# Latent attention: ScalarE copies a turn's probabilities ahead of the next chunk's exponentials; the output stage sums its squares amid the first tile's products

## The reference

```python
s = jnp.einsum('bhqd,bhkd->bhqk', qb, kh) * scale
s = jnp.where(key_idx[None, :] <= q_idx[:, None], s, -jnp.inf)
p = jax.nn.softmax(s, axis=-1)
return jnp.einsum('bhqk,bhkd->bhqd', p, vh)
```

```python
mixed = jnp.concatenate([rms_norm_2(attn, attn_out_norm), rms_norm_2(lru, lru_out_norm)], axis=-1)
x = x + gate1 * (mixed @ w_out)
```

## Time and profile before

| | |
|---|---|
| median of 3 runs | 3761.67 us (3759.36 to 3768.54) |
| the profiled execution's own time | 3749.46 us |
| its span in the trace | 3747.6 us |
| PE busy | 3513.6 us, 94% |
| VectorE busy | 1692.7 us, 45% |
| ScalarE busy | 1037.1 us, 28% |
| GpSimd busy | 988.4 us, 26% |
| latent attention, 2352 to 2768 us: PE busy | 391.20 of 416 us |
| GpSimd busy in the same stretch | 220.10 of 416 us |
| first experts' gather after routing | 3106.49 us |

### The profile page before, as it was taken

One profiled execution on the slowest core, in us unless ns is written; L12 is line 12 of the kernel. 1 busy time (PEld: TensorE's weight loads), 2 busy tenths in 40 slices (PEclk: granted clock), 3 DMA queues, 4 the chain that ended last, 5 costly groups with the idle time before them and its releaser, 6 DMA issues. The chain is left out here.

```text
span 3747.6 us, 33237 instructions
## 1 busy us (share of the span) xinstructions
PE 3513.6 (94%) x11453; PEld 1838.4 (49%) x11453; DVE 1692.7 (45%) x4081; ACT 1037.1 (28%) x2543; POOL 988.4 (26%) x1362
## 2 busy tenths in 40 slices
PE   4999999999999999999999989999989978999997
PEld 3754455555445544444444445555555544444443
DVE  4666433343354763346665557443444452221221
ACT  3122222211100550012244446433322222222221
POOL 0277777500000780000000006555520001112111
PEclk7999999999999999999999989999999988999999
DMA  3134445434253103232211000001012226999997
GB/s 137 58 128 147 164 147 167 152 99 134 91 179 130 35 24 129 84 122 69 94 42 35 12 11 1 1 1 68 1 58 96 74 93 250 323 329 333 332 326 234
DMA packets 115563, 459.96 MB, mean 123 GB/s; under 512 B 13587, under 2 KB 41107, under 8 KB 103356
## 3 DMA queue, kind: packets, MB, share of 16 engines
q1 hardware_dynamic: 91484, 370.18, 27.9%
q0 software_dynamic: 18432, 67.12, 6.4%
q10 hardware_dynamic: 5472, 20.45, 1.5%
HBM read 340.28 MB, written 117.42 MB: 122 GB/s over the span
## 5 line engine op out<-in xcount | busy, mean ns | idle before, releaser
L142 PE MATMUL pst<-arena 128*128 128x512 f32 (+5 forms) x6938 | 2754.0, 555 | 68.0 <-DVE arena L158 34.1
L142 PEld LDWEIGHTS pst<-arena 128*128 128x128 f32 x6938 | 1300.0, 198 | 1399.2 <-issue 1244.3
L164 POOL TENSOR_TENSOR arena<-arena 128x4 f32<-128x4 f32 (+7 forms) x784 | 412.7, 526 | 465.3 <-DVE arena L2043 404.9
L164 DVE TENSOR_TENSOR arena<-arena 128x1 f32<-128x1 f32 (+8 forms) x1260 | 445.4, 354 | 95.3 <-ACT arena L2273 20.2
L147 PE MATMUL pst<-arena 128*128 128x128 f32 x2145 | 322.2, 289 | 119.6 <-DVE arena L246 52.5
L147 PEld LDWEIGHTS pst<-arena 128*128 128x128 f32 x2145 | 257.0, 147 | 276.9 <-issue 148.3
L1286 POOL TENSOR_SCALAR arena<-arena 128x384 f32<-128x384 f32 (+1 forms) x128 | 151.7, 1213 | 523.8 <-DVE arena L1278 522.6
L153 ACT ACTIVATE arena<-pst,arena 128x128 f32<-128x128 f32 (+1 forms) x630 | 244.8, 485 | 112.7 <-PE pst L147 112.7
L2220 POOL TENSOR_SCALAR arena<-arena 128x512 f32<-128x512 f32 (+3 forms) x160 | 219.1, 1393 | 172.5 <-DVE arena L164 158.4
L167 DVE TENSOR_SCALAR arena<-arena 128x1 f32<-128x1 f32 (+11 forms) x581 | 141.2, 243 | 180.7 <-DMA arena<-in_bc 69.1
L173 ACT ACTIVATE arena<-arena 128x1024 f32<-128x1024 f32 x48 | 50.7, 1057 | 599.2 <-DVE arena L1538 342.1
(11 more groups left out here) (194 smaller groups left out, 2105.1 us busy)
## 6 DMA issues: line engine op xcount, KB each, us to landing
arena<-in_w_exp SPq DMA_DIRECT2D x48, 3072.0 KB, 11.9
arena<-in_w_ada SPq DMA_DIRECT2D x48, 512.0 KB, 4.9
rotd<-arena POOLq DMA_DIRECT2D x32, 512.0 KB, 4.0
arena<-rotd SPq DMA_DIRECT2D x32, 512.0 KB, 4.9
arena<-sgd SPq DMA_DIRECT2D x16, 1024.0 KB, 6.8
arena<-pwd SPq DMA_DIRECT2D x32, 416.0 KB, 5.7
pwd<-arena SPq DMA_DIRECT2D x16, 576.0 KB, 5.2
h2d<-arena SPq DMA_DIRECT2D x17, 512.0 KB, 2.9
```

The source lines that it names most:

```text
L142: x = t.do.matmul(o, l, r, start=(i == 0), stop=(i == len(pairs) - 1))
L164: own(v, s).tensor_tensor(o, a, b, op).then_inc(*inc(s, *event))
```

## The change

In `ac_mla`, ScalarE no longer does a score's exponentials where the list has them: it holds them until the next item. If that item is a score or an odd turn, the held exponentials go first, as before. If it is an even turn that doesn't need that score (it never does, for the 39 even turns that follow a score directly), the turn's copy goes first and the exponentials after it.

In `te_o2`, the one-column sums of tile 0 stand between its attention products and its recurrent products, and no longer behind both.

```diff
         def ac_mla(a):
             a.wait_ge(*at("qk_pe", "r", NT - 1))
             qk_done(a)
+            held = []
             for kind, n in ORDER:
                 if kind == "score":
-                    ac_mla_score(a, n)
+                    for m in held:
+                        ac_mla_score(a, m)
+                    held = [n]
                 else:
-                    if n % 2 == 0:
+                    own_scores = SCORE_AT[2 * TURNS[n][0] + 1, chunks_of(2 * TURNS[n][0] + 1) - 1]
+                    late = bool(held) and held[0] > own_scores
+                    if n % 2 == 0 and late:
+                        any_mla_turn(a, n)
+                    for m in held:
+                        ac_mla_score(a, m)
+                    held = []
+                    if n % 2 == 0 and not late:
                         any_mla_turn(a, n)
                     if n >= 2 and TURNS[n - 2][1:] == (1, MJOBS[TURNS[n - 2][0]][1]):
                         any_mla_out(a, TURNS[n - 2][0], 1)
...
                         mm(t, bank(2 * c), [(qn[:, k, tk_], WO2[c][:, k, :]) for k in range(4)])
+                    if i == 0:
+                        te_o2_sums(t, 0)
                     t.wait_ge(*at("ld_mL", "mL", 3))
                     for c in range(2):
                         mm(t, bank(2 * c + 1), [(mL[k][:, tk_], WO2[c][:, 4 + k, :]) for k in range(4)]
                            ).then_inc(*inc("o2_pe", "x3", i, c))
-                    if i == 0:
-                        te_o2_sums(t, 0)
```

## The result

The changed kernel takes 3740.58 us, median of 5 runs (3737.07 to 3742.87), against 3761.67 us before, in the same series 3756.12 to 3768.54. The ratio is 0.9938, with a 95% interval of 0.9917 to 0.9959: 21 us by the medians, 15 to 31 us by the interval. The interval excludes no change, so the kernel became faster; the forecast was 3735.6 us.

The account below looks back on a forecast made before the run. The prediction took TensorE, busy 94% of the span, as the bound. From the 3761.7 us median it subtracted 22.6 us in attention and 3.5 us in the output stage, giving 3735.6 us, range 3729 to 3743.

Parts of the forecast that it names:

- Time won reaches the end: From attention and the output stage through routing to the experts: a microsecond won on TensorE is one at the end.
- Part 1: In latent attention, moving 39 ScalarE copies ahead of exponentials removes TensorE's waits: 22.6 us won, between 18 and 24.8.
- The doubt about GpSimd's 22.9 us: In attention, the list names GpSimd for 22.9 us of TensorE's weight-load waits; the prediction doubted that.
- the slack behind them: In attention, held exponentials have some 5 us before the score after next needs them, so delay costs nothing.
- the three waits beside the scaling: In attention, where VectorE scales output weights: of 4.3 us in three waits, 2.1 come back, bounds 0.9 and 4.3.
- Part 2: In the output stage, moving tile 0's sums between its products wins 3.5 us, between 1.8 and 6.9.
- I take 3.4: In the output stage, the price of products at half clock behind the moved sums: 3.4 us, from half of 6.60.
- The stall: Before tile 1 of the output stage: TensorE's 4.86 us wait plus 2.03 us of slowed products, 6.9 us together.
- The clock stays high: Rival for the output stage: no half clock, so the sums' move wins 6.9 us; 29.5 in all, 3732 us; chance 7%.
- the next wait takes over: Rival in attention: GpSimd or VectorE's odd copies hold turns; about half returns, 14.8 us in all, 3747 us; chance 12%.
- Hardly anything reaches the end: Rival: attention's waits move elsewhere or the expert stage takes the gain back, total within 11 us; chance 7%.
- the slower case: Rival in attention: held exponentials become the path, 39 copies of 0.59 us lose 23 us, 3781 us; chance 2%.

Follow-up runs that it names:

- att_only: The changed kernel with tile 0's sums back where they stood before, so only ScalarE's copies moved: 3744.89 us against 3767.94 for the kernel before, ratio 0.9944.
- split_early: The changed kernel with sums of tiles 0, 2, 6 and 10 in small groups between products and VectorE's output-weight scaling earlier: 3720.28 us against 3763.58 before.
- sums_split: The changed kernel with the one-column sums of tiles 0, 2, 6 and 10 in two or four groups between full-width products: 3723.39 us, ratio 0.9891 to before.
- scale_early: The changed kernel with VectorE's scaling of the output weights from turn 102 instead of 114 and its inverse root at turn 12: 3731.35 us, ratio 0.9906.
- held_late: The changed kernel with three unread 512-column ScalarE copies added between each of 39 moved copies and its exponentials: 3739.18 us, ratio 0.9928 to before.
- before_again: The kernel before, unchanged, run for a second profile: 3764.88 us for the one run.

## Why the prediction was right, step by step

**Time won reaches the end: right.** The att_only run wins 23 us at the end where its stage wins 23.1, split_early 43 where its stages win 47. The total of the change, 21 us by the medians, is less than the 29.0 us of the stages. The interval includes both, and the first part and the last (652 to 665 us in these profiles) scatter by more than the difference. That the missing 8 us are such scatter is likely, not shown. The total came 5 us short of the forecast gain of 26.1 while the stages exceeded it by 3, so the closeness of 3740.6 to 3735.6 is in part luck.

**Part 1: right, 23.1 us for 22.6.** All 25 waits went, the one at 2687 us as well, which the list had put down to GpSimd. The doubt about GpSimd's 22.9 us was right for the larger part: that line fell to 9.2 with the copies. What the 9.2 are stays open; they hold back no matmul. So an engine that is named as the releaser may just have had the nearest event in time. The held exponentials cost nothing, but the slack behind them was right for wide scores only.

The terms inside it were off in both directions. For the three waits beside the scaling I took 2.1 us; between turns 114 and 127 the kernel before takes 34.01 us and the one after 32.58, so 1.4 came. That leaves 21.7, where 20.5 were counted for the other 22 waits. Of the 1.2 us between them, 0.5 were won before the first turn and are none of the change's doing: the third score fell into a stretch at half clock for longer in before than in after. This is that score in before, and then in after:

```profile
2357.76 2.78 PE L2232 MATMUL pst<-arena 128*128 128x384 f32 x4
```

```profile
2373.75 2.24 PE L2232 MATMUL pst<-arena 128*128 128x384 f32 x4
```

The 22 waits themselves gave 21.1 by the start times, 0.03 us more for each than the 0.17 that was added to its printed idle time.

**Part 2: the mechanism right, the size wrong, 5.9 us for 3.5.** The wait of 4.86 us went whole, and the clock fell with TensorE busy, as the rows on the later sums had it and against the Trainium skill (TensorE: Matmul & The Clock Gate, section "Why this matters for your kernels"), which has such drops come from idle gaps. sums_split shows it from the other side: the same sums in smaller groups, and no fall. The failed step is the term "I take 3.4" for half clock. It stood for half of 6.60 us, and the stretch was 3.4 us long, which costs 1.7. A second error lay in the cost of before. The stall was priced at 4.86 + 2.03 = 6.9 us, but the clock was already at half in the last 1.5 us of the sums, and the 4.2 us taken for them is that slowed run; at the full clock they take 3.6. By sums_split the undisturbed tiles take 31.1 us, so before had lost 7.6. The two errors, 1.7 and 0.7, make up the 2.4 us. The scale_early run, with a stretch of 6.8 us, puts the stage at 34.5 and the gain at 4.2 us, so the size of this part depends on which stretch an execution gets.

**The rivals.** "The clock stays high" fell to the stretch at 0.52, "the next wait takes over" to the list of waits: 2.5 us of new waits, not 11. "Hardly anything reaches the end" fell to att_only, and the slower case to held_late, as far as this change goes.

## What to carry to other kernels

On an engine that works in order, put the short instruction that releases the busiest engine ahead of a long one that waits for something later anyway; its price is the slack of the long one's reader, and that is smallest where the tiles are narrow. Break up runs of very narrow matmuls with full-width ones, and look for the half clock in stretches where TensorE is fully busy too. When two profiles are compared, cut both at the same instructions before the spans are believed.

## What the runs showed of the hardware

- Sixteen one-column matmuls in a row, 3.6 us at the full clock, came with a stretch of 6.8 or 10.2 us at half clock where they stood at a tile's end, and with 3.4, once 6.8 and once no time at all where they stood amid a tile's products. The stretch began up to 1.5 us before their end or up to 1.7 us behind it. In groups of 1.8 us and less (sums_split and split_early) they came with none in sixteen tiles. TensorE was busy without a gap except where VectorE held up tile 1 (before, before_again, att_only). What chooses between 3.4, 6.8 and 10.2 stays open.
- ScalarE had 76 us of added work put ahead of exponentials that TensorE needs (held_late), and attention grew by 6.0, of which up to 1.7 are the clock's.
- The same program's first part ended 9 us apart in two profiles, with a wait of 7.2 us for a transfer (arena<-pwd) in one and not in the other.
